# State-space tables with one operand of each pass in PSUM, and shared rotary keys turned once

## The chip, the cores and the metric

One core of a Trainium2 chip runs the whole program in one launch. The metric is the device time in microseconds, before as the median of three runs. TensorE multiplies matrices into PSUM (eight banks of 128 x 512 float32), VectorE and ScalarE work on SBUF and PSUM, GpSimd (POOL) on SBUF, and SyncE issues most of the DMAs.

## The reference, cut to what matters

The reference runs two blocks over 512 tokens of width 1024. The first has a mixer of chunked attention beside a diagonal state-space model (32 groups of 16 channels, 64 complex states each), then memory attention and a product-key feed-forward. The second has two layers with feed-forwards, a differential and stick-breaking mixer in the first layer, and latent attention in the second.

The state-space part needs the discretised eigenvalue `a = exp(lambda * step)` and its powers:

```python
mag = jnp.exp(lr * step)
ar = mag * jnp.cos(li * step)
ai = mag * jnp.sin(li * step)
...
_, _, xr, xi = lax.associative_scan(_complex_affine_combine, (a_r, a_i, bu_r, bu_i), axis=1)
```

The latent attention has 16 heads of 96 dimensions. The last 32 dimensions of a key come from the token alone and are the same in all heads, before the norm of each head:

```python
k_rope = jnp.broadcast_to(dkv[:, None, :, MLA_KV_RANK:], (b, MLA_HEADS, s, MLA_ROPE_DIM))
k = jnp.concatenate([k_nope, k_rope], axis=-1)
q = rms_norm(q, qk_norm_q)
k = rms_norm(k, qk_norm_k)
q = jnp.concatenate([q[..., :MLA_NOPE_DIM], rope(q[..., MLA_NOPE_DIM:])], axis=-1)
k = jnp.concatenate([k[..., :MLA_NOPE_DIM], rope(k[..., MLA_NOPE_DIM:])], axis=-1)
```

`rope` turns pairs of dimensions by an angle that depends on the token.

## The kernel before, in words

Activations are kept with features on the 128 partitions and the 512 tokens along the free dimension. Each stage is a block with a program for every engine, and the next block starts when all engines have ended the one before.

**Weights in pages.** Weights stream from HBM as pages of 128 x 1024 into a ring of seven slots (L179). ScalarE writes the rounded high part of a page (`high_part`, L190), GpSimd subtracts it from the page to get the low part (`low_parts`, L196), and TensorE makes each product of three matmuls, low by high, high by low, high by high (`in_parts`, L427 to L429; L599 to L602 for blocks of tokens). A page becomes free when TensorE has used it, so ScalarE's and GpSimd's work on later pages is paced by TensorE.

**`project`.** A projection goes through `uses`, one output block of 128 features by 512 tokens each, in banks 0 to 5 in turn; bank 7 has the sums for the norm of the input and bank 6 the inverse root spread over the partitions, which ScalarE copies to `small` (`scaled`). VectorE evicts each bank, multiplied by that root (`times`, L1945; `times_by_chunks`, L1980; `times_token`, L1952). TensorE may be six banks ahead of the evictions. A generator given as `beside` is worked on by VectorE between evictions: ahead of each use after the first, `some(budget)` takes steps until the costs that they yield reach 5.2 us; ahead of the first block of tokens it takes 3.5 budgets; what remains runs after the last eviction. Two more calls, `some(12.0)` and `some(4.0)`, stand around the roots at the start of the first projection.

**`turn_tables`** is the generator of the first projection: 17 small instructions, powers 1 to 8 of the eigenvalue by `turn` (six passes: four products, a difference and a sum), the factors of the input; then for 8 levels of `into` and 9 levels of `outof` three passes of 128 x 512 (L379 and L382 products with a factor repeated over 16 columns, L385 their sum), after which `tables_made` is signalled. Then come the cosines and sines of 64 chunks, doubled in number six times by `turn` (L321 to L331, seven calls, since the last doubling is in two halves) with small doublings of the angle between them (`double`, L391 to L394), and `rate` (L415). Every step is chained to the one before by `link`, a semaphore wait. All operands and outputs lie in SBUF.

**After the projection** `state_chunks` begins with 16 transposes of `into` on TensorE (L1378), then products with the rearranged input (L1391). That input is written to HBM after four uses and loaded back by eight DMAs (L1997), which SyncE issues after the last page and when the tables are made.

**Latent attention.** One projection makes the compressed queries `CQ`, the compressed keys and values, and `KR`, with the 32 shared dimensions in partitions 64 to 95 (L2121). A second makes the values, a third (`project(H, MH, 4, ...)`, L2136) all 16 query heads. Then for each half of eight heads: `add_shared` makes the keys (L2133, L2134 adds `KR`), `head_norm` normalises eight query and eight key heads and turns them, and `attention` follows.

**`head_norm`** takes 16 units. ScalarE squares each, TensorE sums them over partitions with a window of `mats` that puts the sum of unit u in rows 2u and 2u + 1 (L798), ScalarE and VectorE take the root. Then for each unit TensorE spreads the root (L812) into one of three banks, VectorE weighs the head by it and by the gain (L843), TensorE multiplies the head by the matrix ROT96 (L819), VectorE multiplies that by the sines (L855) and the head by the cosines (L857), and adds the two (L851).

Of the kernel before, what the change touches and what calls it, by code (L numbers as in the profile page):

```python
# [16 lines left out]
ALU = mybir.AluOpType  # L17
# [3 lines left out]
P = 128  # L21
# [20 lines left out]
ONES, WINDOW, IDENT, ROT64, ROT96, MINUS_TRI, LATER, IOTA = range(8)  # L42
PAIR, ALL = 0, 64
N_MATS = 8
# [26 lines left out]
def build(nc, pages_dram, mats_dram, cols_dram, x_dram, mem_dram, bias_dram, rope_dram, ssm_dram,  # L71
          lam_dram, keys_dram, vecs_dram, spread_dram, groups_dram, u_dram, y_dram, gate_dram, acts_dram, out, cols,
          n_pages):
    with ExitStack() as ctx:
# [232 lines left out]
        def turn_tables(link):  # L307
# [65 lines left out]
            link.eng.wait_ge(ahead.sem, ahead.at(16))  # L373
            a, b = wide(groups, 16)
            for first, other, by_first, by_other, out, order in (
                    (raw_b, other_b, in_re, in_im, into, [(7 - j, j) for j in range(8)]),
                    (raw_c, other_c, power_re, power_im, outof, [(l, l) for l in range(9)])):
                for l, at in order:
                    link(nc.vector.tensor_tensor(a, first, by_first[:, l, :][:, :, None].broadcast_to([P, groups, 16]),  # L379
                                                 ALU.mult))  # L380
                    yield cost(512)
                    link(nc.vector.tensor_tensor(b, other, by_other[:, l, :][:, :, None].broadcast_to([P, groups, 16]),  # L382
                                                 ALU.mult))
# [14 lines left out]
            for level in range(3):  # L398
                yield from double()
            link(nc.vector.tensor_scalar(sin, sin, gcol("sign"), None, ALU.mult))  # L400
            link(nc.vector.memset(cosines[:, :, 0:1], 1.0))
            link(nc.vector.memset(sines[:, :, 0:1], 0.0))
            yield 0.6
            m = 1
            while m < n_chunks:
                w = min(groups, 512 // m)
                for g in range(0, groups, w):
                    c_, s_ = cosines[:, g:g + w], sines[:, g:g + w]
                    by = [x[:, g:g + w][:, :, None].broadcast_to([P, w, m]) for x in (cos, sin)]
# [71 lines left out]
        def project(src, high, nk, n, parts, by="act", norms=None, split=True, squares=None, early=2, keep=None,  # L481
                    fetch=None, at_start=False, beside=None, budget=5.2, also=None, between_pages=None, gelu=None, gated=None):

# [34 lines left out]
            with nc.Block() as block:  # L518
# [17 lines left out]
                def _(pe):  # L536
# [23 lines left out]
                    for part, c in zip(parts, counts):  # L560
                        if part[0] == "features":
                            tiles = part[1] * nk
                            for b in range(part[1]):
                                for j, (k0, k1) in enumerate(segments):
# [193 lines left out]
        def head_norm(units, width, rope=None, at=(0, 3584), newton=newton):  # L758
# [9 lines left out]
            mean = newton[0:32, 0, :]  # L768
            count = len(units)
            long = [unit[0][0].shape[1] for unit in units]  # L770
            with nc.Block() as block:  # L771
# [21 lines left out]
                def _(pe):  # L793
                    for u, (chunks, window, gain) in enumerate(units):
                        pe.wait_ge(squared.sem, squared.at(u + 1))
                        for c in range(len(chunks)):

                            last = nc.tensor.matmul(bank[0][0:32, 0:long[u]],  # L798
                                                    mats[:, WINDOW, window + 30 - 2 * u:window + 62 - 2 * u],
                                                    sq[:, u % 2, c, 0:long[u]], start=(u == 0 and c == 0),  # L800
# [22 lines left out]
                def _(dve):  # L823
# [41 lines left out]
            if rope is not None:  # L865
                for s in (rotated, turned, copied):
                    s.close(count)

# [1062 lines left out]
        def H(k):  # L1931
            return hT[:, k, :]
# [199 lines left out]
        def add_shared(b, ps, link):  # L2132
            link(nc.vector.tensor_tensor(MK(b), ps, r_kv, ALU.mult))  # L2133
            return nc.vector.tensor_tensor(MK(b), MK(b), KR, ALU.add)  # L2134

        project(H, MH, 4, SEQ, [("features", 16, times(Q))], norms=normed(CQ, "mla_q_norm", 512, 4), squares=room(0),  # L2136
                fetch=(hT[:, 6:8, :], rope_dram[1]))
        cosT, sinT = H(6), H(7)
# [15 lines left out]
def _lay_out(a):  # L2154
# [68 lines left out]
    w = f("mla_w_dkv_2")[0]  # L2223
    tiles(w, [(0, slice(0, 128)), (0, slice(128, 256)), (64, slice(256, 288))])
    w = f("mla_w_ukv_2")[0].reshape(256, 16, 128)
# [13 lines left out]
    i = np.arange(P)  # L2239
    mats[:, ONES] = 1  # L2240
    mats[:64, WINDOW, PAIR + 30] = 1
    mats[64:, WINDOW, PAIR + 31] = 1
    mats[:, WINDOW, ALL + 30:ALL + 32] = 1
    mats[:, IDENT] = np.eye(P)
# [55 lines left out]
    column("mla_qk_norm_q", f("mla_qk_norm_q_2")[0], 32)  # L2300
    column("mla_qk_norm_k", f("mla_qk_norm_k_2")[0], 32)
    table = np.ascontiguousarray(np.stack(table).T)
# [44 lines left out]
```

## Time and profile before

| what | value |
| --- | --- |
| median of three runs | 4905.6 us |
| lowest and highest | 4897.28 and 4909.03 us |
| the profiled execution | 4905.1 us, its span 4903.0 us |
| TensorE busy | 4626.3 us, 94% of the span |
| VectorE, ScalarE, GpSimd busy | 42%, 30%, 38% |
| mean granted TensorE clock | 0.97 |

Busy time says how long an engine worked. A stretch in which TensorE has nothing is found by the timeline, and what it waited for by the releaser in square brackets.

### The profile page before, as it was taken

The page shows a single profiled execution, that of the slowest core. Times are in us where ns is not written, and L with a number is a line of the kernel's source. Part 1 is how long each engine was busy: PE and PEld are TensorE (multiplying, and loading weights), DVE is VectorE, ACT ScalarE, POOL GpSimd, SP SyncE. Part 2 cuts the span into 40 slices and gives each one's busy share as a digit, 9 for nine tenths or more (in the row PEclk, how much of TensorE's full clock was granted, in tenths as well). Part 3 has the DMA queues.
Part 4 walks back from the last instruction along what each step waited for, and adds up shares of the span by engine and source line. Part 5 has one row for each costly group of instructions (what it writes and reads, how often), then busy time and mean ns, then how long its engine had stood idle before and what let it go on. Part 6 is the DMA issues. An engine that isn't in the chain of part 4 may idle for free. (4 is left out here: it accounts for less than half of the span.)

```text
span 4903.0 us, 51563 instructions
## 1 busy us (share of the span) xinstructions
PE 4626.3 (94%) x19960; PEld 3546.2 (72%) x19960; DVE 2071.6 (42%) x4317; ACT 1462.9 (30%) x2188; POOL 1843.1 (38%) x820
## 2 busy tenths in 40 slices
PE   7688899999999999999999989899999997798999
PEld 6447578888888888887887746578878873365887
DVE  8564359933332333334431152444144146644440
ACT  2143323344443111112222234432232232244221
POOL 3014144466665444444444301244444430022443
PEclk9789999999999999999999989999999999999999
DMA  3213124454555655563222201122222220011222
GB/s 135 39 42 105 43 95 135 136 168 161 181 182 185 193 185 193 185 193 128 94 95 97 86 3 39 65 90 95 95 91 95 95 86 30 18 59 58 95 95 82
DMA packets 220706, 520.43 MB, mean 106 GB/s; under 512 B 25648, under 2 KB 91568, under 8 KB 217520
## 3 DMA queue, kind: packets, MB, share of 16 engines
q1 hardware_dynamic: 135984, 450.03, 28.0%
q10 hardware_dynamic: 84480, 67.12, 4.4%
q8 instruction: 159, 2.61, 0.2%
q14 instruction: 83, 0.68, 0.1%
HBM read 445.77 MB, written 71.30 MB: 105 GB/s over the span
## 5 line engine op out<-in xcount | busy, mean ns | idle before, releaser
L196 POOL TENSOR_TENSOR ring_rounded<-ring,highs_rounded 128x1024 fp32r<-128x1024 f32 x687 | 1683.5, 2452 | 2911.4 <-ACT highs_rounded L190 2911.4
L427 PE MATMUL bank<-arena_rounded,ring_rounded 128*128 128x512 f32 (+1 forms) x4488 | 1789.6, 399 | 86.1 <-DVE hT_rounded L445 42.8
L429 PE MATMUL bank<-arena_rounded,highs_rounded 128*128 128x512 f32 (+1 forms) x4488 | 1775.5, 396 | 0.0
L190 ACT ACTIVATE highs_rounded<-ring 128x1024 fp32r<-128x1024 f32 x687 | 727.6, 1060 | 2056.9 <-PE bank L429 1610.1
L428 PE MATMUL bank<-hT_rounded,highs_rounded 128*128 128x512 f32 x3128 | 1228.0, 393 | 0.0
L427 PEld LDWEIGHTS bank<-arena_rounded,ring_rounded 128*128 128x128 f32 x4488 | 853.3, 190 | 278.2 <-issue 83.0
L429 PEld LDWEIGHTS bank<-arena_rounded,highs_rounded 128*128 128x128 f32 x4488 | 852.0, 190 | 204.9
L428 PE MATMUL bank<-arena_rounded,highs_rounded 128*128 128x512 f32 (+1 forms) x2112 | 820.2, 388 | 0.0
L428 PEld LDWEIGHTS bank<-hT_rounded,highs_rounded 128*128 128x128 f32 x3128 | 592.7, 189 | 141.5
L428 PEld LDWEIGHTS bank<-arena_rounded,highs_rounded 128*128 128x128 f32 x2112 | 401.6, 190 | 86.7
L1309 DVE TENSOR_TENSOR arena<-qT,arena 128x512 f32<-128x512 f32 x64 | 150.6, 2354 | 372.2 <-ACT qT L1274 371.6
L1863 DVE TENSOR_SCALAR arena<-mats,arena 128x128 f32<-128x128 f32 x512 | 154.5, 410 | 344.0 <-PE bank L1672 344.0
L1755 ACT ACTIVATE arena<-bank 128x512 f32<-128x512 f32 x128 | 76.6, 598 | 480.5 <-PE bank L429 480.5
L423 DVE CAST arena_rounded<-arena 128x512 fp32r<-128x512 f32 x128 | 54.7, 428 | 384.4 <-PE bank L429 384.4
L427 PE MATMUL bank<-qT_rounded,ring_rounded 128*128 128x512 f32 x512 | 203.2, 397 | 0.0
L1316 DVE SCALAR_TENSOR_TENSOR xT<-bank,xT 128x512 f32<-128x512 f32 x32 | 22.1, 692 | 423.3 <-PE bank L429 423.2
L429 PE MATMUL bank<-qT_rounded,highs_rounded 128*128 128x512 f32 x512 | 199.7, 390 | 0.0
L905 PE MATMUL bank<-kT,qT 128*128 128x256 f32 (+7 forms) x384 | 145.1, 476 | 20.6 <-PEq L771 20.6
L1877 DVE TENSOR_TENSOR arena<-arena 128x512 f32<-128x512 f32 x128 | 99.6, 778 | 147.4 <-DMA arena<-gate_table 142.8
L1001 ACT ACTIVATE arena<-bank,small 128x256 f32<-128x256 f32 (+3 forms) x144 | 73.4, 510 | 268.3 <-DVE small L959 267.4
L1723 ACT ACTIVATE qT<-bank 128x512 f32<-128x512 f32 x128 | 134.6, 1131 | 23.0 <-PE bank L1672 22.9
L1672 PEld LDWEIGHTS bank<-arena 128*128 128x128 f32 x1024 | 125.9, 191 | 5.9
(326 smaller groups left out, 4373.8 us busy)
## 6 DMA issues: line engine op xcount, KB each, us to landing
ring<-pages_in SPq DMA_DIRECT2D x687, 512.0 KB, 3.3
act_table<-arena SPq DMA_DIRECT2D x128, 256.0 KB, 3.9
gate_table<-qT SPq DMA_DIRECT2D x16, 2048.0 KB, 7.2
arena<-act_table ACTq DMA_DIRECT2D x128, 256.0 KB, 4.0
arena<-gate_table ACTq DMA_DIRECT2D x32, 1024.0 KB, 8.2
arena<-mem_in SPq DMA_DIRECT2D x3, 1024.0 KB, 4.8
arena<-spread_in SPq DMA_DIRECT2D x5, 512.0 KB, 4.5
xT<-x_in SPq DMA_DIRECT2D x8, 256.0 KB, 6.0
```

The costliest lines, as they stand in the source:

```text
L190: nc.scalar.activation(f32r(page_high(p)), slot(p), ACT.Copy).then_inc(masked_pages.sem, 1)
L196: nc.gpsimd.tensor_tensor(f32r(slot(p)), slot(p), part_of(page_high(p)), ALU.subtract).then_inc(split_pages.sem, 1)
L427: low_last = nc.tensor.matmul(out, f32r(w_low), f32r(x_high), start=start, stop=False)
L428: nc.tensor.matmul(out, f32r(w_high), f32r(x_low), start=False, stop=False)
L429: return low_last, nc.tensor.matmul(out, f32r(w_high), f32r(x_high), start=False, stop=stop)
L905: last = nc.tensor.matmul(bank[u % 3][:, 0:span[qb]], q[c][:, qb * P:qb * P + P], k[c][:, 0:span[qb]], start=(c == 0), stop=(c == len(q) - 1))
L1309: nc.vector.tensor_tensor(w_low(f), w_high(f), up_scaled, ALU.mult).then_inc(made2.sem, 1)
L1672: last = nc.tensor.matmul(bank[4 + b][:, k * P:k * P + P], one1[:, b, k, :], one2[:, b, k, :], start=True, stop=True)
L1723: nc.scalar.activation(wide[:, h % 2, :, k * quad:k * quad + quad].rearrange("p j t -> p t j"), bank[4 + q % 4][:].rearrange("p (t j) -> p ...
L1755: nc.scalar.activation(kept[:, r % 2, :], bank[r % 2][:], ACT.Gelu).then_inc(made.sem, 1)
L1863: last = nc.vector.tensor_scalar(one1[:, b, k, :], iota, turnedT[:, 1, t:t + 1], turnedT[:, 0, t:t + 1], ALU.is_equal, ALU.mult)
L1877: nc.vector.tensor_tensor(raw[:, r % 3, :].rearrange("p (h t) -> p h t", h=n_half), acts_in[:, b, :].rearrange("p (h t) -> p h t", h=n_hal ...
```

## The change

**Tables.** In `turn_tables` the scratch `a` of the big passes moves to bank 6 and the scratch `b` stays in SBUF (`wide_in_bank`). The factors of eight levels, 128 x 256, are copied to bank 7 ahead of each table (four copies), and the products read them there; the ninth level of `outof` reads its factors in SBUF. For the cosines and sines the present angle's cosine and sine are copied to bank 7 (`cos_now`, `sin_now`, 12 copies of 128 x 32), and `turn` uses bank 6 for `a`. The generator waits for `scaled` ahead of the big passes. The assumed cost of a step falls from 0.25 + 1.6e-3 a column to 0.25 + 1.1e-3, which changes how many steps `some` takes.

**Rotary keys.** The gain of the shared dimensions is applied to `KR` once and `KR` is turned once, while the queries are projected (`turn_shared`, beside; `turn_product`, one product into bank 7 after use 5). The weights put the shared dimensions a second time in partitions 96 to 127, where they stay unturned, and the window `SHARED` sums the squares of partitions 0 to 63 and 96 to 127. The query heads are zero in the partitions from 96 up. `head_norm` gets a number of units to turn: eight of 16, the queries.

```diff
             def cost(n):
-                return 0.25 + n * 1.6e-3
-
-            def turn(out_re, out_im, re, im, by_re, by_im, w, m):
+                return 0.25 + n * 1.1e-3
+
+            in_bank = (bank[6][:], rows[1])
+
+            def wide_in_bank(w, m):
+                return [r[:, 0:w * m].rearrange("p (a b) -> p a b", a=w) for r in in_bank]
+
+            def turn(out_re, out_im, re, im, by_re, by_im, w, m, wide=wide):
...
             link.eng.wait_ge(ahead.sem, ahead.at(16))
-            a, b = wide(groups, 16)
+            link.eng.wait_ge(scaled.sem, scaled.at(1))
+            a, b = wide_in_bank(groups, 16)
...
+                banked = [bank[7][:, 256 * j:256 * j + 256].rearrange("p (l g) -> p l g", l=8) for j in range(2)]
+                for to, x in zip(banked, (by_first, by_other)):
+                    link(nc.vector.tensor_copy(to, x[:, 0:8, :]))
+                    yield cost(256)
                 for l, at in order:
-                    link(nc.vector.tensor_tensor(a, first, by_first[:, l, :][:, :, None].broadcast_to([P, groups, 16]),
+                    c, d = (banked if l < 8 else (by_first, by_other))
+                    link(nc.vector.tensor_tensor(a, first, c[:, l, :][:, :, None].broadcast_to([P, groups, 16]),
                                                  ALU.mult))
...
+            cos_now, sin_now = bank[7][:, 0:32], bank[7][:, 32:64]
...
             while m < n_chunks:
+                link(nc.vector.tensor_copy(cos_now, cos))
+                link(nc.vector.tensor_copy(sin_now, sin))
+                yield 0.3
...
                     yield from turn(c_[:, :, m:2 * m], s_[:, :, m:2 * m], c_[:, :, 0:m], s_[:, :, 0:m],
-                                    by[0], by[1], w, m)
+                                    by[0], by[1], w, m, wide_in_bank)
...
                                     between(use)
+                                    if product is not None and use == 5:
+                                        product(pe)
...
-                        if rope is not None and u >= 1:
+                        if 1 <= u <= turns:
...
-                    for u in range(count + (3 if rope is not None else 0)):
+                    for u in range(max(count, turns + 3 if turns else 0)):
...
-                        if rope is not None and u >= 3:
+                        if 3 <= u < turns + 3:
...
-                        if rope is not None and 2 <= u < count + 2:
+                        if 2 <= u < turns + 2:
...
+        scaled_kr = arena[:, 7680:8192]
+
+        def turn_shared(link):
+            link(nc.vector.tensor_scalar(scaled_kr, KR, gcol("mla_k_rope"), None, ALU.mult))
+            link.eng.sem_inc(made.sem, 1)
+            for j in range(6):
+                yield 6.0
+            link.eng.wait_ge(ahead.sem, ahead.at(16))
+            link.eng.wait_ge(rotated.sem, rotated.at(1))
+            here = slice(64, 96)
+            link(nc.vector.tensor_tensor(KR[here], bank[7][here, :], sinT[here], ALU.mult))
+            link(nc.vector.tensor_tensor(scaled_kr[here], scaled_kr[here], cosT[here], ALU.mult))
+            link(nc.vector.tensor_tensor(KR[here], KR[here], scaled_kr[here], ALU.add))
+            yield 2.0
+
+        def turn_product(pe):
+            pe.wait_ge(made.sem, made.at(1))
+            pe.wait_ge(inverted.sem, inverted.at(1))
+            nc.tensor.matmul(bank[7][:], mat(ROT96), scaled_kr, start=True, stop=True).then_inc(rotated.sem, 1)
...
             head_norm([([Q(8 * half_ + h)], ALL, "mla_qk_norm_q") for h in range(8)]
-                      + [([MK(h)], ALL, "mla_qk_norm_k") for h in range(8)], 96,
-                      rope=(ROT96, cosT, sinT))
+                      + [([MK(h)], SHARED, "mla_qk_norm_k") for h in range(8)], 96,
+                      rope=(ROT96, cosT, sinT, 8))
```

## Rows read from the trace of the kernel before

**Rows 1.** The page, part 1: busy us, share of the span, instructions.

```profile
PE 4626.3 (94%) x19960; PEld 3546.2 (72%) x19960; DVE 2071.6 (42%) x4317; ACT 1462.9 (30%) x2188; POOL 1843.1 (38%) x820
```

**Rows 2.** Timeline, tables' ends and what follows: start us, us, engine, line.

```profile
29.69 0.09 DVE L338 MEMSET arena<- 128x32 f32 x1
...
146.54 0.09 DVE L416 MEMSET arena<- 128x32 f32 x1
147.16 3.72 PE L1378 MATMUL bank<-mats,arena 128*128 128x128 f32 x16 [22.94 <-PEq L518]
```

**Rows 3.** Windows: us, busy us (PE, PEld, DVE, ACT, POOL), PEclk, DMA share, GB/s.

```profile
132.00:134.00 2.00, 0.00 (x0) 0.00 (x0) 2.00 (x4) 0.00 (x0) 0.00 (x0) 0.50 1.43 107
134.00:136.00 2.00, 0.00 (x0) 0.00 (x0) 1.90 (x5) 0.00 (x0) 0.00 (x0) 0.50 0.93 67
```

**Rows 4.** Groups of instructions by line, VectorE, first 140 us.

```profile
L382 DVE TENSOR_TENSOR arena<-qT,arena 128x512 f32<-128x512 f32 x17 | 17.1, 1003 | 0.5
L385 DVE TENSOR_TENSOR arena<-arena 128x512 f32<-128x512 f32 x17 | 16.4, 966 | 0.4
L379 DVE TENSOR_TENSOR arena<-qT,arena 128x512 f32<-128x512 f32 x17 | 16.3, 958 | 0.4
...
L1980 DVE TENSOR_TENSOR kT<-bank,small 128x512 f32<-128x512 f32 x4 | 4.4, 1099 | 0.1
```

**Rows 5.** Timeline of VectorE and GpSimd during the tables.

```profile
37.08 2.47 DVE L325 TENSOR_TENSOR arena<-arena 128x128 f32<-128x128 f32 x1
...
83.17 2.77 DVE L382 TENSOR_TENSOR arena<-qT,arena 128x512 f32<-128x512 f32 x1
...
113.78 0.21 DVE L327 TENSOR_TENSOR arena<-qT,arena 128x32 f32<-128x32 f32 x1
114.02 2.39 DVE L329 TENSOR_TENSOR arena<-qT,arena 128x32 f32<-128x32 f32 x1
...
119.59 2.33 DVE L393 TENSOR_SCALAR arena<-arena 128x32 f32<-128x32 f32 x1
...
82.98 2.41 POOL L196 TENSOR_TENSOR ring_rounded<-ring,highs_rounded 128x1024 fp32r<-128x1024 f32 x1 [3.17 <-ACT highs_rounded L190]
88.55 2.36 POOL L196 TENSOR_TENSOR ring_rounded<-ring,highs_rounded 128x1024 fp32r<-128x1024 f32 x1 [3.16 <-ACT highs_rounded L190]
```

**Rows 6.** Groups of instructions by line, VectorE, whole span.

```profile
L1309 DVE TENSOR_TENSOR arena<-qT,arena 128x512 f32<-128x512 f32 x64 | 150.6, 2354 | 372.2 <-ACT qT L1274 371.6
...
L1316 DVE SCALAR_TENSOR_TENSOR xT<-bank,xT 128x512 f32<-128x512 f32 x32 | 22.1, 692 | 423.3 <-PE bank L429 423.2
```

**Rows 7.** Timeline of the first `head_norm` of the latent attention.

```profile
4120.59 0.74 DVE L843 SCALAR_TENSOR_TENSOR kT<-kT,col,bank 128x512 f32<-128x512 f32 x1
...
4123.05 0.74 DVE L843 SCALAR_TENSOR_TENSOR kT<-kT,col,bank 128x512 f32<-128x512 f32 x1
...
4126.30 1.12 PE L819 MATMUL bank<-kT,mats 128*128 128x512 f32 x2 [0.48 <-DVE kT L843]
...
4141.77 0.69 DVE L851 TENSOR_TENSOR kT<-kT,arena 128x512 f32<-128x512 f32 x1
4143.06 1.19 PE L905 MATMUL bank<-kT,qT 128*128 128x128 f32 x3 [5.79 <-PEq L771]
```

**Rows 8.** Window in the second part of that `head_norm`, columns as in rows 3.

```profile
4120.00:4137.00 17.00, 12.80 (x27) 4.05 (x25) 17.00 (x29) 0.00 (x0) 0.00 (x0) 1.00 0.00 1
```

**Rows 9.** Timeline of VectorE in the first attention, a pass into a bank.

```profile
254.42 0.70 DVE L955 TENSOR_TENSOR bank<-bank,arena 128x512 f32<-128x512 f32 x1 [0.60 <-PE bank L905]
255.20 0.11 DVE L958 MEMSET bank<- 64x64 f32 x1
```

**Rows 10.** Timeline of SyncE, the loads of the rearranged input.

```profile
124.23 6.32 SPq L1997 DMA_DIRECT2D qT<-u_table  x8
```

**Rows 11.** One line's instructions, L855: durations, first and last start.

```profile
L855 DVE TENSOR_TENSOR arena<-bank,hT x32: 680/682/684, 4104.6 to 4284.0; 128x512 f32<-128x512 f32 x32
```

**Rows 12.** Timeline of VectorE in the query projection.

```profile
4033.31 0.69 DVE L1945 TENSOR_TENSOR qT<-bank,small 128x512 f32<-128x512 f32 x1 [2.10 <-PE bank L429]
```

More of the change, by code:

```diff
@@ L42 @@
 ONES, WINDOW, IDENT, ROT64, ROT96, MINUS_TRI, LATER, IOTA = range(8)
-PAIR, ALL = 0, 64
+PAIR, ALL, SHARED = (WINDOW, 0), (WINDOW, 64), (ONES, 64)
 N_MATS = 8
@@ L377, in turn_tables @@
                     (raw_c, other_c, power_re, power_im, outof, [(l, l) for l in range(9)])):
+                banked = [bank[7][:, 256 * j:256 * j + 256].rearrange("p (l g) -> p l g", l=8) for j in range(2)]
+                for to, x in zip(banked, (by_first, by_other)):
+                    link(nc.vector.tensor_copy(to, x[:, 0:8, :]))
+                    yield cost(256)
                 for l, at in order:
-                    link(nc.vector.tensor_tensor(a, first, by_first[:, l, :][:, :, None].broadcast_to([P, groups, 16]),
+                    c, d = (banked if l < 8 else (by_first, by_other))
+                    link(nc.vector.tensor_tensor(a, first, c[:, l, :][:, :, None].broadcast_to([P, groups, 16]),
                                                  ALU.mult))
                     yield cost(512)
-                    link(nc.vector.tensor_tensor(b, other, by_other[:, l, :][:, :, None].broadcast_to([P, groups, 16]),
+                    link(nc.vector.tensor_tensor(b, other, d[:, l, :][:, :, None].broadcast_to([P, groups, 16]),
                                                  ALU.mult))
@@ L408, in turn_tables @@
                     c_, s_ = cosines[:, g:g + w], sines[:, g:g + w]
-                    by = [x[:, g:g + w][:, :, None].broadcast_to([P, w, m]) for x in (cos, sin)]
+                    by = [x[:, g:g + w][:, :, None].broadcast_to([P, w, m]) for x in (cos_now, sin_now)]
                     yield from turn(c_[:, :, m:2 * m], s_[:, :, m:2 * m], c_[:, :, 0:m], s_[:, :, 0:m],
-                                    by[0], by[1], w, m)
+                                    by[0], by[1], w, m, wide_in_bank)
                 m *= 2
@@ L481, in project @@
         def project(src, high, nk, n, parts, by="act", norms=None, split=True, squares=None, early=2, keep=None,
-                    fetch=None, at_start=False, beside=None, budget=5.2, also=None, between_pages=None, gelu=None, gated=None):
+                    fetch=None, at_start=False, beside=None, budget=5.2, also=None, product=None, between_pages=None, gelu=None, gated=None):
             first = page.start
@@ L769, in head_norm @@
             count = len(units)
+            turns = (rope[3] if len(rope) > 3 else count) if rope is not None else 0
             long = [unit[0][0].shape[1] for unit in units]
@@ L798, in _ @@
                             last = nc.tensor.matmul(bank[0][0:32, 0:long[u]],
-                                                    mats[:, WINDOW, window + 30 - 2 * u:window + 62 - 2 * u],
+                                                    mats[:, window[0], window[1] + 30 - 2 * u:window[1] + 62 - 2 * u],
                                                     sq[:, u % 2, c, 0:long[u]], start=(u == 0 and c == 0),
@@ L866, in head_norm @@
                 for s in (rotated, turned, copied):
-                    s.close(count)
+                    s.close(turns)
         def attention(heads, nkeys, causal, bias=None, prob=None, turned_at=1536, table_at=5632):
@@ L2134, in add_shared @@
             return nc.vector.tensor_tensor(MK(b), MK(b), KR, ALU.add)
+        scaled_kr = arena[:, 7680:8192]
[15 more added lines that the diff above has]
+            nc.tensor.matmul(bank[7][:], mat(ROT96), scaled_kr, start=True, stop=True).then_inc(rotated.sem, 1)
+        cosT, sinT = H(6), H(7)
         project(H, MH, 4, SEQ, [("features", 16, times(Q))], norms=normed(CQ, "mla_q_norm", 512, 4), squares=room(0),
-                fetch=(hT[:, 6:8, :], rope_dram[1]))
-        cosT, sinT = H(6), H(7)
+                fetch=(hT[:, 6:8, :], rope_dram[1]), beside=turn_shared, product=turn_product)
+        made.close(1)
+        rotated.close(1)
         for half_ in range(2):
@@ L2223, in _lay_out @@
     w = f("mla_w_dkv_2")[0]
-    tiles(w, [(0, slice(0, 128)), (0, slice(128, 256)), (64, slice(256, 288))])
+    tiles(np.concatenate([w, w[:, 256:288]], 1), [(0, slice(0, 128)), (0, slice(128, 256)), (64, slice(256, 320))])
     w = f("mla_w_ukv_2")[0].reshape(256, 16, 128)
@@ L2239, in _lay_out @@
     i = np.arange(P)
[L2240 to L2243, printed above, removed]
+    mats[:, ONES, 0] = 1
+    mats[:64, WINDOW, PAIR[1] + 30] = 1
+    mats[64:, WINDOW, PAIR[1] + 31] = 1
+    mats[:, WINDOW, ALL[1] + 30:ALL[1] + 32] = 1
+    mats[:64, ONES, SHARED[1] + 30:SHARED[1] + 32] = 1
+    mats[96:, ONES, SHARED[1] + 30:SHARED[1] + 32] = 1
     mats[:, IDENT] = np.eye(P)
@@ L2300, in _lay_out @@
     column("mla_qk_norm_q", f("mla_qk_norm_q_2")[0], 32)
-    column("mla_qk_norm_k", f("mla_qk_norm_k_2")[0], 32)
+    k_gain = f("mla_qk_norm_k_2")[0]
+    column("mla_qk_norm_k", np.concatenate([k_gain[:64], np.ones(32, np.float32)]), 32)
+    column("mla_k_rope", np.concatenate([np.zeros(64, np.float32), k_gain[64:]]), 32)
     table = np.ascontiguousarray(np.stack(table).T)
```

## The prediction

> **What bounds the kernel now.** I read the page's first part, then windows and the timeline, then the groups of instructions. TensorE is busy for 94% of the span [rows 1], so only stretches in which it stands still and waits for something can give time back. The change touches two such stretches.
>
> The first is the making of the state-space tables. VectorE starts them at 29.69 us and ends them at 146.54 + 0.09 us; TensorE's next matmul is at 147.16, after 22.94 us of standing still [rows 2]. The window from 132 to 134 has no matmul and 2.00 us of VectorE in 2 [rows 3]. In those 117 us VectorE hardly pauses: its length of work is the length of the stage. The reader should see in the groups that the three passes of the big tables (L379, L382, L385) have means of 958 to 1003 ns [rows 4], while a pass of that size with both inputs in SBUF takes 0.69 us where GpSimd is idle, as L851 does [rows 7]. The timeline says why: GpSimd's subtraction of a page runs from 82.98 for 2.41 us, and the pass that VectorE issues at 83.17 takes 2.77 us, ending about 0.5 us after it [rows 5]. So a VectorE instruction whose operands all lie in SBUF stands still while GpSimd works. An instruction with one operand in PSUM does not: over the whole kernel L1309, two SBUF inputs beside GpSimd, has a mean of 2354 ns, and L1316, a bank and xT in the same part of the kernel, 692 [rows 6].
>
> The second is `head_norm` of the latent attention, twice. There one head costs VectorE four passes in 2.46 us (4120.59 to 4123.05), the last of them begins at 4141.77, and TensorE starts the attention at 4143.06 [rows 7]. VectorE has 17.00 us of work in 17, at a granted clock of 1.00 (2.4 GHz) [rows 8]: VectorE bounds it.
>
> **Tables: what goes.** The three groups hold 17.1 + 16.4 + 16.3 = 49.8 us for 51 passes [rows 4]; at L851's 0.69 they would be 35.2. So 14.6 us are waits for GpSimd. One pass of the sine tables, L329 at 114.02, takes 2.39 where its neighbour of that size takes 0.21: 2.2 more [rows 5]. Together 16.8 us in passes that the change gives a PSUM operand. Four more stalls of about 2.1 us, the first at 37.08 and the last at 119.59 [rows 5], are in instructions that stay in SBUF, 8.5 us together. They don't all stay: a pass now counts as 0.81 and not as 1.07, so `some(5.2)` takes seven passes where it took five, and GpSimd, paced by TensorE's pages, meets other instructions. Walking the new order against page subtractions 5.6 us apart (82.98 and 88.55 [rows 5]), I get two stalls, 4.0 us; but the small doublings could be met again. I take 4 off, with 0 and 6.4 as ends. Only two passes of the ninth level (`l == 8`) still have two SBUF inputs; one more stall, 2.1, is the bad end there.
>
> **Tables: what comes.** The trace has no copy from SBUF to a bank. A 128x32 pass takes 0.21 [rows 5] and a 128x512 one 0.69 [rows 7], which puts a 128x256 one at 0.43; four such copies. Twelve copies of 128x32 at 0.21. What writes to a bank hands on later: L955 lasts 0.70 and the next instruction starts 0.78 after it [rows 9], a gap of 0.08, where the chained passes have 0.5 us of gaps in 17 [rows 4], 0.03 each. The sixteen copies thus cost 4 x 0.51 + 12 x 0.29 = 5.5, and the 31 passes that write to the bank (17, and two in each of 7 turns) 31 x 0.05 = 1.6. In all 7.1 us. Low end: 4.4, with copies at half that price; high end 9, with the twelve small ones at 0.45 each, as a 256-wide one.
>
> The Trainium skill, in "SBUF — State Buffer", Who interferes with whom, says that a VectorE instruction with at most one SBUF input, outside the modes that use both ports, does not contend with GpSimd; by that rule the trace agrees, and the copies into the bank would be free of stalls too.
>
> Sum of the tables: -16.8 - 4 + 7.1 = -13.7 us; ends -16.8 - 6.4 + 4.4 = -18.8 and -16.8 + 2.1 + 9 = -5.7.
>
> **Does it reach TensorE?** Two things could end later than VectorE. The projection's last matmul ends at 147.16 - 22.94 = 124.2 [rows 2], and TensorE has waited for evictions before that; with evictions of seven passes (5.1 us) plus 0.6 to 1.0 each, against a page period of 5.6, its last four uses wait less, and by the same walk it ends near 120.5. VectorE asks for the token blocks only about 6 us later. The eight loads of the rearranged input are issued from 124.23, behind the last page [rows 10], and the DMA share falls from 1.43 to 0.93 in the window to 136 [rows 3], so they land some 11.5 us after TensorE's end. Then 132, while the first product that reads them comes behind 16 transposes, 3.72 us [rows 2], after the new start of about 133.4, at 137. Both are hidden, with 5 us left; cover gone, the first microsecond lost would be the one beyond that. `some(4.0)` now reaches the waits for `ahead` and `scaled` before the first eviction; that eviction waits for `scaled` anyway, and the input asked for was loaded long before, so nothing is queued behind it that ran earlier.
>
> **Heads: what goes.** Of 16 units, 8 keep the turn. For each of the others three of four passes go, 24 in each half, 48 in the 2 halves (the line L855 shows 32 of them from 4104.6 to 4284.0, 16 a half [rows 11]). The walk: until unit 10, at 4123.05, nothing changes; its pass and one addition end near 4124.4, five more weighings at 0.74 give 4128.1 instead of 4141.77 + 0.69 = 4142.46. TensorE must feed them: a product is two instructions, 1.12 us from first to end in the row of L819 [rows 7], of which I count 0.86 as the step to the next, with three banks ahead; five units by that are 4.3 against 3.7, so 4128.1 to 4128.7. I take 14.3 for each half, 28.6. At the lower clock level (1.2 GHz) a unit is 1.7, and each half would give 4 less: bad end 20; good end 29.4.
>
> **Heads: what comes.** One product with ROT96 in the query projection. There VectorE waits 2.10 us for TensorE before an eviction of 0.69 [rows 12], so TensorE sets the pace and the product is on the path: about 1.0 us by L819. The shared gain pass falls behind the first eviction and ahead of those that are queued by then; even stalled by GpSimd they are done when TensorE wants their banks, six uses later. The three 32-row passes at use 7, some 2 to 4.5 us, delay one eviction and are made up in 2.10 us gaps. Nothing else waits for them. The rotation's product is issued after use 5, before VectorE asks. Loads, pages, squares and matmuls of the sums stay the same in number. Sum: -27.6; ends -28.6 and -18.
>
> **Together** -13.7 - 27.6 = -41.3. The profiled execution lasted 4905.1 (span 4903.0), within 0.5 us of the runs' median of 4905.6, so 4905.1 - 41.3 = 4863.8: I say 4864.
>
> **The rivals.**
> 1. PSUM does not keep a pass off GpSimd's way. Then the tables give nothing and cost 7.1: 4905.1 + 7.1 - 27.6 = 4885. For it: no row shows a pass with a PSUM output and an SBUF input together with GpSimd. Against: L1316 at 692. Chance 0.07.
> 2. Passes with a PSUM source have a longer start. L843, which reads a bank, takes 0.74 and L851 without one 0.69 [rows 7]; 0.05 us on 91 passes is 4.6: 4868. Against: L1316 also reads a bank and takes 692 ns [rows 6]. Chance 0.07. The Trainium skill, "VectorE: DVE Perf Modes", the section on the TRN2 errata, gives a fixed cost of 120 cycles for PSUM to SBUF against 58; by that rule a pass would take 0.065 us more, an estimate, and the time would be 4870; L1316 does not agree with it.
> 3. Slower: a chained pass through a bank, written and read at once by the same engine, takes twice as long, 1.38. 68 passes of 512 elements lose 0.69, 47, and 24 shorter ones 0.2, 5: -41.3 + 52 = +11, 4916. It decides from 0.61 us more a pass. For it: only L1980, a bank operand with a scattered output, at 1099 ns [rows 4]; at that price (+0.41) it is 4895. Against: L955, bank to bank, 0.70. Chance 0.02, and 0.03 for 4895.
> 4. The heads become bound by TensorE, because its clock is low in the second part: 20 and not 28.6, 4872. Against: 1.00 in that window. Chance 0.08.
> 5. The tables' gain stops at the loads: if they land at 141 instead of 132, because the projection ends no earlier and its last page delays them too, 4 us are lost: 4868. Chance 0.06.
>
> My own case has 0.67. Faster by over 0.3% (about 15 us, what a measurement of this kernel can tell from no change) is all but rival 3 and a little of the first: 0.94; within 0.3% 0.04; slower 0.02. The range takes cases 2, 4 and 5. Both good ends together, 18.8 + 28.6, give 4858; one bad end with the other term as forecast gives 4872 (tables) or 4873 (heads). The runs shown lie up to 8 us below their median and 3 above; with some of that, 4853 to 4876.
>
> **What would show it.** Right: L379, L382 and L385 at 0.69 to 0.72 mean; evictions of uses 6 to 9 earlier; VectorE's last table pass near 133, TensorE's transposes near 133.4; 16 passes of L855's line in the latent attention instead of 32, and each of its `head_norm`s 14 us shorter; one product more in the query projection. Wrong: passes over 2 us beside GpSimd in those lines; durations above 0.8 at 512 elements; a wait of the products of `state_chunks` for a DMA; weighings of units 11 to 15 spaced by more than 0.9.

## The result, and the profile after

The changed kernel takes 4838.36 us (median of 4 runs, 4831.89 to 4841.78), the kernel before beside it 4904.06 (4 runs): a ratio of 0.9863, with a 95% interval of 0.9848 to 0.9877. That is 66 us gained where I forecast 41, and 15 us under my range. The profiled executions differ by as much: spans of 4835.2 and 4903.0.

First the page of the changed kernel, part 1 (busy us, share of the span, instructions), against [rows 1].

```profile
PE 4585.4 (95%) x19930; PEld 3549.5 (73%) x19930; DVE 2027.9 (42%) x4289; ACT 1463.2 (30%) x2188; POOL 1843.1 (38%) x820
```

VectorE has 43.7 us less to do. TensorE has 40.9 us less too, with 30 instructions fewer of 19960, the rotation products of the shared keys. At 1.12 us for two [rows 7] these are 17 us; the other 24 are the first sign of something that I had not costed, since shorter waits leave the busy time alone.

The stretch behind the tables: the timeline of TensorE and SyncE in the changed kernel (start us, us, engine, line; the count is of instructions).

```profile
130.04 4.02 PE L1396 MATMUL bank<-mats,arena 128*128 128x128 f32 x16 [7.72 <-PEq L533]
136.87 7.06 PE L1409 MATMUL bank<-qT,arena 128*128 128x64 f32 x32 [2.81 <-DMA qT<-u_table]
143.72 1.92 PE L1396 MATMUL bank<-mats,arena 128*128 128x128 f32 x8
145.43 3.80 PE L1409 MATMUL bank<-qT,arena 128*128 128x64 f32 x32
149.06 1.05 PE L1396 MATMUL bank<-mats,arena 128*128 128x128 f32 x8
149.94 7.26 PE L1409 MATMUL bank<-qT,hT 128*128 128x64 f32 x64
...
122.31 7.28 SPq L2015 DMA_DIRECT2D qT<-u_table  x8
```

And the same stretch in the kernel before:

```profile
150.72 3.68 PE L1391 MATMUL bank<-qT,arena 128*128 128x64 f32 x32
...
155.12 3.68 PE L1391 MATMUL bank<-qT,arena 128*128 128x64 f32 x32
...
159.52 7.26 PE L1391 MATMUL bank<-qT,hT 128*128 128x64 f32 x64
```

The transposes start at 130.04 instead of 147.16 [rows 2], 17.1 us earlier; 1.2 of these the changed kernel already had at ScalarE's L627 (24.1 us in the kernel before), ahead of any table. The reader should then compare the starts of the last rows: 149.94 against 159.52, only 9.6 us earlier. So 7.5 us are given back within 20. The row at 136.87 shows both ways. TensorE waits 2.81 us for the load of the rearranged input, and the 32 products then take 7.06 where they took 3.68. The windows (columns as in rows 3) tell why. Changed kernel:

```profile
130.00:150.00 20.00, 17.04 (x97) 16.17 (x98) 4.00 (x6) 5.47 (x13) 0.00 (x0) 0.61 0.35 23
150.00:170.00 20.00, 20.00 (x131) 19.28 (x131) 9.96 (x13) 1.94 (x5) 0.00 (x0) 0.73 0.00 1
```

Kernel before:

```profile
150.00:170.00 20.00, 20.00 (x181) 19.94 (x179) 12.79 (x16) 4.93 (x13) 0.00 (x0) 0.99 0.01 2
```

The granted clock was 0.61 and 0.73 in the mean over these windows, so TensorE ran for a part of them at 1.2 GHz and for a part at 2.4, where the kernel before had 0.99.

The tables themselves, in the groups of VectorE from 0 to 92 us of the changed kernel, with different shapes kept apart:

```profile
L396 DVE TENSOR_TENSOR arena<-bank,arena 128x512 f32<-128x512 f32 x17 | 11.7, 689 | 0.5
L390 DVE TENSOR_TENSOR bank<-qT,bank 128x512 f32<-128x512 f32 x16 | 11.2, 699 | 0.5
L393 DVE TENSOR_TENSOR arena<-qT,bank 128x512 f32<-128x512 f32 x16 | 11.0, 686 | 0.5
L393 DVE TENSOR_TENSOR arena<-qT,arena 128x512 f32<-128x512 f32 x1 | 2.7, 2703 | 0.0
L386 DVE COPY bank<-arena 128x256 f32<-128x256 f32 x4 | 1.8, 441 | 0.1
```

Means of 686 to 699 ns against 958 to 1003 [rows 4]. Two passes of the ninth level read SBUF alone. The timeline has them one behind the other:

```profile
86.88 0.70 DVE L390 TENSOR_TENSOR bank<-qT,arena 128x512 f32<-128x512 f32 x1
87.61 2.70 DVE L393 TENSOR_TENSOR arena<-qT,arena 128x512 f32<-128x512 f32 x1
```

The first had begun 0.17 us before GpSimd's subtraction (87.05 to 89.77) and ran on at 0.70; the second, issued in the middle of it, took 2.70. One case doesn't tell whether the first was spared by its start or by its output in the bank.

The first `head_norm` of the latent attention in the changed kernel, to set against [rows 7]:

```profile
4091.19 0.73 DVE L861 SCALAR_TENSOR_TENSOR kT<-kT,col,bank 128x512 f32<-128x512 f32 x1
4091.85 0.68 DVE L869 TENSOR_TENSOR qT<-qT,arena 128x512 f32<-128x512 f32 x1
4092.45 1.39 DVE L861 SCALAR_TENSOR_TENSOR kT<-kT,col,bank 128x512 f32<-128x512 f32 x2
4094.09 0.75 DVE L861 SCALAR_TENSOR_TENSOR kT<-kT,col,bank 128x512 f32<-128x512 f32 x1 [0.25 <-PE bank L830]
4095.42 1.60 DVE L861 SCALAR_TENSOR_TENSOR kT<-kT,col,bank 128x512 f32<-128x512 f32 x2 [0.58 <-PE bank L830]
...
4097.64 1.54 PE L923 MATMUL bank<-kT,qT 128*128 128x128 f32 x6 [1.40 <-PEq L789]
```

Units count from 0, and the pass of unit 10 is at 4091.19, in the kernel before at 4123.05 [rows 7]. From there to the attention's first product it is 6.45 us where it was 20.01: 13.6 less. The product's line in the kernel before:

```profile
4143.06 2.90 PE L905 MATMUL bank<-kT,qT 128*128 128x128 f32 x6 [5.79 <-PEq L771]
```

In the second half TensorE comes late with the last roots. A window and two rows of the timeline of VectorE:

```profile
4217.60:4225.00 7.40, 5.49 (x6) 1.81 (x7) 4.93 (x8) 0.00 (x0) 0.00 (x0) 0.54 0.00 0
...
4222.24 0.75 DVE L861 SCALAR_TENSOR_TENSOR kT<-kT,col,bank 128x512 f32<-128x512 f32 x1 [0.96 <-PE bank L830]
4223.95 0.75 DVE L861 SCALAR_TENSOR_TENSOR kT<-kT,col,bank 128x512 f32<-128x512 f32 x1 [0.96 <-PE bank L830]
```

At a granted clock of 0.54 the last weighings stand 1.71 us apart, and unit 10 to the attention is 7.38 us where it was 19.72: 12.3 less.

Now the sum of the way. I set corresponding instructions of ScalarE side by side; the lead of the changed kernel is 7.7 us at 176 us, 31.5 at 4017, 45.7 at the start of the latent attention, 62.8 after its second half's first scores, and 67.9 at the end. The parts are thus 7.7 (tables), 31.7 from the first sums of squares of the latent attention to those scores (14.1 and 13.6 for the two `head_norm`s up to the attention's first instruction of ScalarE, twice 1.2 for an attention that starts at the higher clock, 1.5 in the sums of squares), and **28.5 us that come bit by bit** in stages that the diff doesn't touch. They don't come evenly: 0.75 for each 77 us from 1000 to 1500, 0.9 for each 225 from 1600 to 2200, and in a few places up to 2.7 are given back. One such stretch, between two instructions of ScalarE of the kernel before, in windows; before, then changed:

```profile
2443.80:2510.70 66.90, 66.90 (x290) 54.06 (x289) 27.63 (x30) 15.85 (x19) 28.74 (x12) 1.00 0.29 95
```

```profile
2443.80:2510.70 66.90, 66.90 (x294) 54.85 (x293) 28.59 (x33) 15.84 (x18) 28.58 (x12) 1.00 0.28 95
```

TensorE is busy throughout in both, at a clock of 1.00, with the same kind of product; in 66.90 us it starts 290 of them before and 294 after. Over each full 100 us of the trace the mean step from one such matmul to the next is 232.2 ns before and 228.9 after in the projections and most of the expert layers, and 233.3 and 232.4 from 1600 to 2200 us. Over the whole trace it is 232.2 and 230.4, and 1.8 ns on some 15,460 steps are about 27 us.

### The profile page after: what moved, and what is told of

Same layout as the page of the kernel before. It is cut to its first block and busy times, and to the rows that moved or that the text cites. A ratio compares the mean times of both kernels' runs of the same rounds, so it can differ in the third digit from the quotient of the medians.

```text
span 4835.2 us, 51463 instructions
## 1 busy us (share of the span) xinstructions
PE 4585.4 (95%) x19930; PEld 3549.5 (73%) x19930; DVE 2027.9 (42%) x4289; ACT 1463.2 (30%) x2188; POOL 1843.1 (38%) x820
```

## The experiments

Eleven more runs, one of them the kernel before once again. In all texts "step" is the mean time from one 512-column product to the next. Each run has the kernel before beside it, and its ratio is against that: 4905.63 us beside the runs of experiments 1 and 2, 4908.19 beside those of 3 and 5, 4909.84 beside those of 4.

**1. The kernel before once more, and each part alone.** `tables_only` has the whole new table code and the planner's new 1.1e-3; `heads_only` has the shared turn alone:

```diff
 # tables_only, of the kernel before
-                return 0.25 + n * 1.6e-3
+                return 0.25 + n * 1.1e-3
...
+                    link(nc.vector.tensor_copy(to, x[:, 0:8, :]))
...
 # heads_only, of the kernel before
-                      + [([MK(h)], ALL, "mla_qk_norm_k") for h in range(8)], 96,
-                      rope=(ROT96, cosT, sinT))
+                      + [([MK(h)], SHARED, "mla_qk_norm_k") for h in range(8)], 96,
+                      rope=(ROT96, cosT, sinT, 8))
...
+    column("mla_k_rope", np.concatenate([np.zeros(64, np.float32), k_gain[64:]]), 32)
```

> The kernel before, unchanged, profiled a second time. In the changed kernel the untouched products of long stages step at 228.9 ns a matmul where the kernel before steps at 232.2, which is worth some 25 of its 66 us. Theory P (the pace is a property of the program: each stage falls into one of several fixed patterns): ratio 1.000 and the trace shows 232.2 ns again in the same stages. Rival C (the pace belongs to the chip or the moment of the profile): the steps come out at 228.9 in some of these stages, and the ratio strays from 1.000 by up to 0.005.

> Only the change to the state-space tables. By the walk of the traces it gives 8 us up to the head norm of the first attention (17 at the end of the tables, of which the wait for the loads and a lower clock take 9 back): 4896. Theory P: what is left over of the 66 us comes from the pace of stages after it, so that this kernel, whose TensorE program is that of the kernel before, shows another pace somewhere between 600 and 3960 us; if the pace is that of the changed kernel, 4874. Rival (the pace comes with the heads' part): 232.2 ns everywhere as before and 4896.

> Only the rotary keys' change. Own gain by the traces 14.3 for each half, 1 to 2 for attentions that start at a higher clock, 1.0 paid for the product: about 29 to 31 us, 4874. Theory P with the tables as trigger: the steps ahead of 3960 us are 232.2 ns as in the kernel before, 4873 to 4876. Rival: the pace comes with the heads' part (other contents of mats, other placement of the program), 228.9 ns ahead of 3960 already, 4850.

Measured: `before_again` 4906.51 us, ratio 1.0002 (0.9992 to 1.0011); `tables_only` 4897.04, 0.9982 (0.9972 to 0.9991); `heads_only` 4848.71, 0.9882 (0.9865 to 0.9898). The parts alone give 9 and 57 us in the medians, and together they make the 66. By the spans it is 7.8 + 51.4 = 59.2 against 67.8. Both parts alone had the lower clock in `state_chunks` in their profiled executions (6.2 us each, experiment 2), and the two together pay for it once; that the medians add up so well may be luck. The step is 232.2 ns in `before_again` and `tables_only` and 228.9 in `heads_only`. So the gain bit by bit comes with the rotary part, and long before the rotary stage.

**2. One more instruction at the end of the tables.** Whether the pace, or the clock of `state_chunks`, hangs on when a stage starts:

```diff
             link(nc.vector.tensor_copy(rate, mag8[:, :, None].broadcast_to([P, groups, n_chunks])))
+            link(nc.vector.tensor_copy(rate, mag8[:, :, None].broadcast_to([P, groups, n_chunks])))
```

> The kernel before with the last copy of the tables (L415, 1.23 us) made twice: VectorE's program is longer by one instruction, and everything behind the tables starts about 1.3 us later. If the pace of later stages hangs on when they begin or on small shifts, some stages change between 228.9 and 232 to 233 ns and the time moves by several us more than the 1.3, either way; if it hangs on what a stage computes or on TensorE's program, all steps stay and the time is 4905.5.

Measured: 4909.72, 1.0009 (0.9999 to 1.0018). The step is 232.2 ns as before, so a mere shift in time doesn't set the pace. Timeline of this kernel:

```profile
147.53 4.02 PE L1379 MATMUL bank<-mats,arena 128*128 128x128 f32 x16 [23.97 <-PEq L519]
151.34 6.93 PE L1392 MATMUL bank<-qT,arena 128*128 128x64 f32 x32
```

The block starts 0.4 us later than before, after 23.97 us of standing still instead of 22.94, and the first 32 products take 6.93 instead of 3.68. The lower clock doesn't need the new tables: `heads_only` has it too, with the old ones (6.93 at 150.24), as have two of the kernels with a shifted memory below. Of the eight profiled executions with the old tables, four do these 32 products in 3.68 or 3.69 us, as the kernel before, and four in 6.92 or 6.93. The standstill doesn't sort them: 22.63 to 22.94 us ahead of those in 3.68, 21.77 to 23.97 ahead of those in 6.93. What tips it stays open, and so does how often the executions without a profile have it. The price is 3.3 us for the first 32 products. From the first transposes to a late instruction of ScalarE (42.4 us in the kernel before) it is 6.2 in `delay_one` and `heads_only`, and 9.1 in the two kernels below where the second 32 products take 6.93 as well; `before_gap_behind_arena` below has 3.69 and loses 3.5 later in the block. All five profiled kernels with the new tables take 6.93 or 7.06.

**3. Where the arena lies.** The diff adds one column, "mla_k_rope", to the table of columns, of 152 before. Tensors are laid one behind another at multiples of 32 bytes, so `col` takes 640 bytes a partition instead of 608, and `arena`, `small` and `params` behind it begin 32 bytes later. This is an unused tensor in the kernel before, and nothing else:

```diff
         col = sb("col", [P, cols_dram.shape[1]])
+        gap = sb("gap", [P, 8])      # before_gap32; [P, 16] in before_gap64
         arena = sb("arena", [P, 18688])
```

and the changed kernel with its column table behind `params` and a gap of the old table's size in its place (`after_old_place`), so that all else lies as before the change.

> The kernel before with an unused tensor of 32 bytes a partition between col and arena. Theory A (address): the rotary change adds one column to col, 152 to 153, so that col needs 640 bytes and not 608 and every tensor behind it (arena, small, params) begins 32 bytes later, at a multiple of 64 bytes a partition instead of 32 beyond one; the matmuls that read arena are faster from there. Then this kernel, with no other change, steps at 228.9 ns where the kernel before steps at 232.2, and takes 4877, up to 4883 if the state chunks start at the lower clock as in the other runs (5.5 us). Rival B (what the mats or the program hold in the changed kernel sets the pace): 232.2 ns and 4905.

> The kernel before with an unused tensor of 64 bytes between col and arena: arena moves on, but stands again 32 bytes beyond a multiple of 64. Theory A with the place modulo 64 as cause: 232.2 ns and 4905. If a mere shift or a bigger distance from the tensors in front is the cause: 228.9 ns and 4877 to 4883.

> The changed kernel with col put behind params and an unused tensor of 608 bytes in its old place: arena, small and params have the addresses that they have in the kernel before. Theory A: the steps return to 232.2 ns and the time rises by the 25 to 28 us that the pace gave, 4863 to 4867, which is where the forecast for the two changes themselves stood. Rival B: 228.9 ns and 4838.

Measured: `before_gap32` 4877.63 us, 0.9936 (0.9919 to 0.9952); `before_gap64` 4914.79, 1.0012 (1.0002 to 1.0022), the 6.92 us of experiment 2 in it; `after_old_place` 4866.08, 0.9912 (0.9895 to 0.9928). The same window in `before_gap32`:

```profile
2443.80:2510.70 66.90, 66.90 (x294) 54.84 (x293) 27.59 (x30) 15.84 (x18) 29.14 (x13) 1.00 0.29 95
```

in `before_gap64`:

```profile
2443.80:2510.70 66.90, 66.90 (x290) 54.01 (x288) 27.64 (x30) 15.83 (x18) 28.75 (x12) 1.00 0.28 95
```

and in `after_old_place`:

```profile
2443.80:2510.70 66.90, 66.90 (x290) 54.06 (x289) 27.63 (x30) 15.83 (x18) 28.75 (x13) 1.00 0.29 95
```

Thirty-two unused bytes give the 294 products; 64 take them back; the changed kernel with the old layout has 290. By spans the 32 bytes are worth 4903.0 - 4872.7 = 30.3 us in the kernel before and 4863.9 - 4835.2 = 28.7 in the changed one. And 4866, 42.1 us under the kernel before beside it, is what the two edits are worth by themselves: my forecast was 4864, a gain of 41.3. In this kernel the lead of ScalarE over the kernel before is 8.4 us at 426 us and still 8.4 at 4030; with the arena in one place, the stages that no edit touches take the same time. It falls by 0.9 at the added rotation product and grows to 39.1 by the end of the two halves.

In the window from 2443.80 the three products of a page's part follow one another, two that read the arena and one that reads hT. The mean steps that begin with the first two are 235.2 and 233.3 ns in the kernel before, 228.3 and 232.3 in `before_gap32`; the step that begins with the one on hT falls as well, from 228.2 to 226.0.

**4. Which tensor it is.** The gap behind the arena moves `small` and `params` alone; gaps of 32 on both sides move the arena by 32 and them by 64; a gap in front of the changed kernel's arena puts it 64 bytes from its old place.

```diff
+        gap = sb("gap", [P, 8])      # before_gap_both; after_gap32, in the changed kernel
         arena = sb("arena", [P, 18688])
+        gap_2 = sb("gap_2", [P, 8])  # before_gap_both; before_gap_behind_arena has this one alone
         small = sb("small", [P, 512])
```

> The kernel before with 32 bytes put behind the arena instead of in front of it: small and params move by 32 bytes, the arena stays. If the start of the arena sets the pace of the products, the mean step stays at 232.2 ns in the tokens' stretch from 600 to 1500 us, and the time at 4905 (ratio 1.000 within 0.0015). If the places of small and params set it, the step is 228.9 ns and the time near 4876. The state chunks' clock may cost 6 us in either case.

> The kernel before with 32 bytes in front of the arena and 32 bytes behind it, so that the arena moves by 32 bytes and small and params by 64. If the start of the arena sets the pace, the mean step is 228.9 ns and the time 4872 to 4880 (ratio 0.993 to 0.995). If small and params set it, they stand as before but for 64 bytes, the step is 232.2 ns and the time 4905 to 4915.

> The changed kernel with 32 bytes put between the column table and the arena, so that the arena, small and params start 64 bytes from where they do before the change; the column table stays in its place. If the start of the arena is what gave the gain beyond the two edits, the step goes back to 232.2 ns and the time to 4864 to 4872 (ratio 0.991 to 0.993). If the place of the column table had a part in it, the time stays nearer to 4838.

Measured: `before_gap_behind_arena` 4907.87 us, 0.9999 (0.9989 to 1.0008), step 232.2; `before_gap_both` 4884.68, 0.9942 (0.992 to 0.9965), step 228.9; `after_gap32` 4876.26, 0.9934 (0.9917 to 0.995), step 232.2. The window again, `before_gap_behind_arena`:

```profile
2443.80:2510.70 66.90, 66.90 (x290) 54.06 (x289) 27.63 (x30) 15.84 (x18) 28.72 (x13) 1.00 0.28 95
```

`before_gap_both`:

```profile
2443.80:2510.70 66.90, 66.90 (x294) 54.79 (x294) 27.67 (x30) 15.83 (x18) 29.02 (x13) 1.00 0.29 95
```

The start of the arena alone sets the pace (`before_gap_both` has the 6.93 us of experiment 2 as well, and its median lies above the 4872 to 4880 that I expected, its ratio inside); the places of `small`, `params` and the column table don't. The two layouts with the arena 64 bytes on are also slower than the old one: steps of 234.3 ns instead of 233.3 from 1600 to 2200 us, and 0.8 ns more from 1000 to 1500. Over the whole trace it is 232.8 against 232.2 in `after_gap32`, some 9 us, and its second 32 products take 6.93 us against 4.33 in `after_old_place`. That is why its time is 10 us longer (14.3 in the spans), outside what I expected of it. Three starts of the arena were tried. Counted by the sizes of the tensors in front of it, the quick one is a multiple of 64 bytes and the other two are 32 beyond one; whether that is the rule, one quick start can't show.

**5. The loads earlier.** The rearranged input asked for three pages earlier, so that rival 5's wait goes:

```diff
-            if i == 15:
+            if i == 12:
```

> The changed kernel with the eight loads of the rearranged input issued after the thirteenth page of the projection instead of the sixteenth. In the changed kernel TensorE waits 2.81 us for them at 134.1 and then does the first products at the lower clock (7.06 us for 32 of them against 3.68 before). If the wait is what keeps the clock low, both go: 4838 - 2.8 - 4 = 4831. If the lower clock comes from the standstill ahead of the block alone, only the wait goes: 4835. If the loads delay a page that TensorE needs, 4838 or more.

Measured: 4834.74 us, 0.9843 (0.9827 to 0.986). Its timeline:

```profile
105.84 7.13 SPq L2015 DMA_DIRECT2D qT<-u_table  x8
...
129.70 4.02 PE L1396 MATMUL bank<-mats,arena 128*128 128x128 f32 x16 [7.07 <-PEq L533]
133.52 6.93 PE L1409 MATMUL bank<-qT,arena 128*128 128x64 f32 x32
140.24 1.92 PE L1396 MATMUL bank<-mats,arena 128*128 128x128 f32 x8
141.94 3.97 PE L1409 MATMUL bank<-qT,arena 128*128 128x64 f32 x32
```

The wait is gone and the first products start 3.35 us earlier (133.52 against 136.87). They still run at the lower clock, so the wait was not what lowered it. This is the shortest time of all, but its interval overlaps that of the changed kernel, and the profiled spans (4835.5 and 4835.2) show no gain at the end: what is won here is not proven to last.

## Why the prediction was wrong

**The step that failed** stands nowhere in a sentence of the prediction and is in its sum: 4905.1 - 41.3, which lets every stage that the diff doesn't name keep its pace. I followed the new column as a gain that VectorE reads, and not as 32 bytes in front of the arena, from which 14174 of the 19960 products of this kernel read. TensorE is busy for 95% of the span, and its step fell from 232.2 to 230.4 ns in the mean: about 27 us by the steps, 29 to 30 by the spans, more than either term that I worked out. That it is the arena's start is shown by experiments 3 and 4: the bytes alone give the gain in the kernel before, and it goes when they are taken from the changed kernel.

The range's lower end, 4853, had no room for it: both good ends, and the spread of the runs. `after_old_place`, the change as I costed it, has 4866. That it comes within 2 us of the forecast is in part luck: by ScalarE's lead over the kernel before the tables gave 8.4 us, 5 less than forecast, and the heads 30.7, 3 more.

**Tables.** Forecast 13.7, measured by `tables_only` 9 in the medians and 7.8 in the spans, within the ends of 5.7 and 18.8. By steps:
- "PSUM operands keep the passes off GpSimd's way": right; 686 to 699 ns, and rival 1 is refuted. The 16.8 us of stalls went. Of the four others I had two left, and one more in the ninth level as the bad end; the timeline shows one of the small passes, 2.38 at 35.84, and one of the ninth level, 2.70 at 87.61, the same two stalls' worth.
- The copies and the later hand-over, 7.1: too dear. A 128x256 copy has a mean of 441 ns, as interpolated, but what comes behind a write to a bank starts about 0.03 us after its end (51.20 + 0.76 to 51.99), not 0.08.
- The block's start, 133.4: it was 130.04, and 1.2 of the 3.4 us are this execution's own. Rival 2 (a longer start with a PSUM source) did not show: 689 ns for a pass from a bank into SBUF. The Trainium skill, "VectorE: DVE Perf Modes", the TRN2 errata, would have these passes 0.065 us longer (an estimate); the trace doesn't agree.
- "Both are hidden, with 5 us left": wrong, and rival 5's mechanism, at 0.06, came in. I had the loads land at 132, 11.5 us behind an end of TensorE's projection at 120.5. That end was 130.04 - 7.72 = 122.3, and from the issue at 122.31 to the products that waited for them, 136.87, it took 14.6 us; and the block came 3.4 us sooner than forecast. Price: 2.81 us.
- Not in my sum at all: the clock of `state_chunks`, 6.2 us. The trace of the kernel before showed it high after 22.94 us of standing still (150.72 + 3.68 for 32 products), and I took that as given. Against `heads_only`, which has the lower clock as well, the tables give 10 us in the medians and 16.4 in the spans (its profiled execution is the slowest of its four).

**Heads.** Forecast 27.6; 30.7 by ScalarE's lead in `after_old_place`, where the arena lies as before. The walk was right in its kind and a little too good: 13.6 and 12.3 us less from unit 10 to the attention, against 14.3 each. "TensorE must feed them" at a step of 0.86 held for some of the weighings only. Rival 4's mechanism, at 0.08, came in at the end of each half: waits of 0.25 and 0.58 in the first, at a granted clock of 0.72 from 4091 to 4097, and of 0.25, 0.96 and 0.96 in the second, at 0.54, with the steps of 1.71 us that I had named as its price. It took under 1 us and 2 us of the 14.3, not 4 from each. This was made up by what I had not looked for: the scores then start at the higher clock (1.00 from 4097.6 to 4101.9 against 0.62 from 4143.0 to 4148.8), 6 matmuls in 1.54 us instead of 2.90, 1.5 us for each half, 1.2 of them behind the attention's first instruction of ScalarE. And the stretches ahead of unit 10 shrink over both halves by 1.5 us in the sums of squares and 1.2 behind them. The one product added costs what I said, about 1.0: the lead of `after_old_place` falls from 8.43 to 7.57 there. In the changed kernel the change of pace hides it.

So the gain was 24 us more than forecast in the medians (65.7 against 41.3) and 26.5 in the spans (67.8). The arena's place gives 24 in the medians (65.7 - 42.1, each against the kernel before beside it) and 28.7 in the spans; the terms that I worked out came to 42.1 in the medians and 39.1 in the spans, with errors of either sign in them.

## What to carry to other kernels

A diff that adds a column, a constant or a buffer moves all that is laid out behind it; before summing an edit, list which tensors move and whether the bottleneck engine reads them. When the bottleneck's own busy time falls without work being removed, look at the mean step of its commonest instruction in a stage that nobody touched, and then put the old layout back under the new code: that one run separated the edit from its address. The block behind a standstill of 22 us ran at either level of the clock here, by 6 to 9 us; price such a block at both.

## What was not expected of the hardware

- The pace of matmuls that read the arena depends on where it starts: 232.2 ns a step in the old place, 228.9 with 32 bytes more, 232.2 with 64 bytes more (234.3 against 233.3 in one part), all at a granted clock of 1.00. Some stretches go the other way: the token blocks from 100 to 125 us (230.0 before, 233.2 after), 3400 to 3500 (231.7 and 232.5), and from 4800 to the end (231.1 and 233.3). No run here shows what inside the chip makes the difference, or whether it is the operand that is streamed or the one that is loaded.
- One more instruction of VectorE, a start 0.4 us later and a standstill 1.0 us longer went with a change from 3.68 to 6.93 us for the same 32 products; gaps in the memory layout did the same in two of four kernels.
- A copy from SBUF to a bank next to a working GpSimd took 441 ns for 128x256 and did not stand still (the copy at 44.00 lay inside GpSimd's work from 43.98 to 46.39); a pass with inputs and output in SBUF in the same stage took 2703.
